# A causal mask added by VectorE in PSUM, in place of two masking products on TensorE

## What is computed

```python
s = jnp.einsum('bnqkgd,bnpkd->bnkgqp', qb, kw, preferred_element_type=F32) * SCALE
...
mask = (diff >= 0) & (diff < WINDOW) & (tk[:, None, :] >= 0)
s = jnp.where(mask[None, :, None, None], s, NEG)
p = jax.nn.softmax(s, axis=-1)
return jnp.einsum('bnkgqp,bnpkd->bnqkgd', p, vw.astype(F32)).reshape(B, S, H, dh)
```

## Time and profile before

| what | value |
|---|---|
| median of 3 runs | 555.83 us (555.33 to 557.75) |
| the profiled execution | 555.62 us, of which the span from first to last instruction is 553.8 us |
| granted TensorE clock over the span | 0.998 |
| TensorE busy | 539.1 us, 97% of the span |
| VectorE busy | 394.7 us, 71% |
| ScalarE busy | 294.2 us, 53% |
| attention, first layer | from about 134 us to 250 us of the span |
| attention, second layer | from about 398 us to 532 us |

### The profile page before, as it was taken

The page is one execution under the profiler, slowest core; times in us unless marked ns, Lnnn a source line. Parts: engine busy times, 40 slices in busy tenths (PEclk is TensorE's granted clock), DMA queues, the critical chain, the costliest instruction groups (busy, mean ns, idle before and its releaser), DMA issues.

```text
span 553.8 us, 8602 instructions
## 1 busy us (share of the span) xinstructions
PE 539.1 (97%) x3171; PEld 400.8 (72%) x3171; DVE 394.7 (71%) x651; ACT 294.2 (53%) x592; POOL 43.7 (8%) x86
## 2 busy tenths in 40 slices
PE   6999999999999999999999999999999999999995
PEld 5777868778767766668887787777877776776674
DVE  4686996689976778656737499668977687587542
ACT  4847735625755465543634773572475454455532
POOL 3001100130000000000520110013000000000000
PEclk9999999999999999999999999999999999999999
DMA  9858465365111111012333856627422112000013
GB/s 265 222 150 212 97 167 109 79 146 137 51 48 30 38 39 40 5 35 76 79 96 95 212 127 152 125 58 151 98 74 78 39 39 49 28 2 1 1 38 113
DMA packets 92040, 49.91 MB, mean 90 GB/s; under 512 B 40912, under 2 KB 90208, under 8 KB 92000
## 3 DMA queue, kind: packets, MB, share of 16 engines
q1 hardware_dynamic: 89376, 45.17, 32.2%
q0 software_dynamic: 1536, 3.15, 2.3%
q10 hardware_dynamic: 1088, 1.06, 0.6%
HBM read 44.12 MB, written 2.10 MB: 83 GB/s over the span
## 4 chain that ended last, share of the span: by engine, by line
PE 77%; DVE 13%; issue 4%; ACT 3%; DMA 1%; POOL 1%; POOLq 0%; DVEq 0%; ACTq 0%
PE z_ps L1491 12%; PE z_ps L1493 11%; PE z_ps L1492 11%; PE t_ps L1591 7%; PE s_ps L1567 6%; PE o_ps L1627 5%; PE a_ps L1627 4%; PE o_ps L1491 3%; PE o_ps L1493 3%; PE o_ps L1492 3%; DVE w_lo L1119 2%; DVE probs L1273 2%; PE t_ps L1601 1%; PE t_ps L1596 1%; DMA swp<-E 1%
## 5 line engine op out<-in xcount | busy, mean ns | idle before, releaser
L1055 ACT ACTIVATE probs<-s_ps,mn 128x128 f32<-128x128 f32 (+3 forms) x128 | 66.6, 526 | 72.1 <-DVE mn L1389 70.7
L1491 PE MATMUL z_ps<-h_hi,w_hi 128*128 128x512 f32 x248 | 101.5, 409 | 1.3 <-issue 0.9
L1493 PE MATMUL z_ps<-h_hi,w_lo 128*128 128x512 f32 x248 | 97.0, 391 | 0.0
L1492 PE MATMUL z_ps<-h_lo,w_hi 128*128 128x512 f32 x248 | 96.8, 390 | 0.0
L900 ACT ACTIVATE w_hi<-stage 128x1024 fp32r<-128x1024 f32 x56 | 59.2, 1058 | 58.7 <-PE z_ps L1493 36.2
L1119 DVE TENSOR_TENSOR w_lo<-stage,w_hi 128x1024 fp32r<-128x1024 f32 x56 | 68.3, 1220 | 7.8 <-ACT w_hi L900 7.0
L1389 DVE TENSOR_REDUCE mn<-s_ps 128x1 f32<-128x384 f32 (+3 forms) x88 | 52.3, 635 | 28.1 <-PE s_ps L1575 27.9
L1491 PEld LDWEIGHTS z_ps<-h_hi,w_hi 128*128 128x128 f32 x248 | 46.6, 188 | 15.5 <-issue 5.5
L1493 PEld LDWEIGHTS z_ps<-h_hi,w_lo 128*128 128x128 f32 x248 | 46.6, 188 | 10.2
L1492 PEld LDWEIGHTS z_ps<-h_lo,w_hi 128*128 128x128 f32 x248 | 46.7, 188 | 8.5 <-issue 0.2
L1398 DVE COPY probsT<-t_ps 128x512 f32<-128x512 f32 (+1 forms) x48 | 32.8, 684 | 22.1 <-PE t_ps L1591 21.8
(11 more groups left out here) (235 smaller groups left out, 915.2 us busy)
## 6 DMA issues: line engine op xcount, KB each, us to landing
stage<-in_w_in SPq DMA_DIRECT2D x28, 512.0 KB, 4.5
stage<-in_w_in SPq DMA_DIRECT2D x32, 256.0 KB, 3.8
stage<-in_cmp_k_w SPq DMA_DIRECT2D x8, 512.0 KB, 3.8
stage<-in_cmp_v_w SPq DMA_DIRECT2D x8, 512.0 KB, 4.2
stage<-in_w_out SPq DMA_DIRECT2D x8, 512.0 KB, 3.5
stage<-in_w_out SPq DMA_DIRECT2D x16, 256.0 KB, 3.8
swp<-E POOLq DMA_DIRECT2D x48, 64.0 KB, 2.3
out<-xT SPq DMA_DIRECT2D x8, 256.0 KB, 2.4
```

Source lines behind the costliest of these rows:

```text
L1055: act.activation(probs[:, 4 * pair + 2 * g + r, c0:c0 + W], s_ps[g][:, at * W:(at + 1) * W], ACT.Exp, scale=-1.0, bias=mn[:, m % 2, g, at: ...
L1491: pe.matmul(bank, w_hi[:, slot, at:at + P], x_hi, start=first, stop=False)
L1492: pe.matmul(bank, w_hi[:, slot, at:at + P], x_lo, start=False, stop=False)
L1493: ins = pe.matmul(bank, w_lo[:, slot, at:at + P], x_hi, start=False, stop=last)
```

## The change

The masking products leave the score step. The last of the three score products now closes the bank and signals VectorE. VectorE adds a table `causal` (128 by 128 float32, zero up to the diagonal and 1e30 beyond) to the last 128 columns of every head in the bank, in place in PSUM, waits for this by a `link`, and then takes the minimum as before. GpSimd builds one table in place of four half tables.

```diff
-        ident_b, causal_b = sb("ident_b", [P, 2, P], BF16), sb("causal_b", [P, 2, P], BF16)
+        causal = sb("causal", [P, P])
...
-        N_CONST = 7
+        N_CONST = 8
...
-            link(pool.memset(ident_b[:, :, :], 0.0))
-            for h in range(2):
-                rows = slice(h * HD, (h + 1) * HD)
-                link(pool.affine_select(out=ident_b[rows, :, :], in_=ident_b[rows, :, :], compare_op=ALU.not_equal, fill=1.0, base=0,
-                                        pattern=[[HD, 2], [-1, P]], channel_multiplier=1))
...
-            link(pool.memset(causal_b[:, :, :], 0.0))
-
-            for h in range(2):
-                rows = slice(h * HD, (h + 1) * HD)
-                link(pool.affine_select(out=causal_b[rows, :, :], in_=causal_b[rows, :, :], compare_op=ALU.is_ge, fill=BIG, base=0,
-                                        pattern=[[HD, 2], [-1, P]], channel_multiplier=1))
+            link(pool.memset(causal[:, :], 0.0))
+
+            pool.affine_select(out=causal[:, :], in_=causal[:, :], compare_op=ALU.is_ge, fill=BIG, base=0,
+                               pattern=[[-1, P]], channel_multiplier=1).then_inc(consts, 1)
...
                 elif kind == "MX":
                     _, l, step, g = st
                     m, many, W = step_no[(l, *step)], len(parts(step)), P * (step[0] + 1)
+                    if g == 0 and m == 0:
+                        dve.wait_ge(consts, N_CONST)
                     if g == 0 and m >= 2:
                         dve.wait_ge(exp_ok, plan.exps[m - 1])
                     dve.wait_ge(s_full, N_KV * m + g + 1)
+                    on_diag = s_ps[g][:, 0:many * W].rearrange("p (h w) -> p h w", h=many)[:, :, W - P:W]
+                    later = causal[:, :].rearrange("p (h c) -> p h c", h=1).to_broadcast([P, many, P])
+                    link(dve.tensor_tensor(on_diag, on_diag, later, ALU.add))
...
-                            pe.matmul(s_ps[g][:, at * wide:(at + 1) * wide], q_st[rows, GROUP * of_q + q, i * P:(i + 1) * P],
-                                      keys, start=(at == 0 and part == 0), stop=False, skip_group_check=True)
-
-                for a in range(2):
-                    for g in range(N_KV):
-                        rows = slice(g * HD, (g + 1) * HD)
-                        diagonal = s_ps[g][:, 0:many * W].rearrange("p (h w) -> p h w", h=many)[:, :, W - P + a * HD:W]
-                        later = causal_b[rows, a, a * HD:P].rearrange("p (h c) -> p h c", h=1).to_broadcast([HD, many, P - a * HD])
-                        ins = pe.matmul(diagonal, ident_b[rows, a, :], later, start=False, stop=(a == 1),
-                                  skip_group_check=True)
-                        if a == 1:
-                            ins.then_inc(s_full, 1)
+                            ins = pe.matmul(s_ps[g][:, at * wide:(at + 1) * wide], q_st[rows, GROUP * of_q + q, i * P:(i + 1) * P],
+                                            keys, start=(at == 0 and part == 0), stop=(part == 2), skip_group_check=True)
+                            if part == 2 and at == len(heads) - 1:
+                                ins.then_inc(s_full, 1)
```

More of the change, by code:

```diff
@@ L1559, in scores @@
                     pe.wait_ge(rope_lo, last + 1)
-                many, wide = len(parts(step)), len(branches) * W
+                wide = len(branches) * W
                 for at, (pair, r) in enumerate(heads):
```

## The result

The changed kernel takes 564.99 us (median of 4 runs, 563.07 to 566.62) against 556.39 us for the kernel before in the same session (4 runs, 555.33 to 557.75). The ratio is 1.015 with an interval of 1.013 to 1.017: slower by 8.6 us, where 5.5 us were forecast. The one run of the changed kernel at a granted clock of 0.999 took 563.07 us; the three other runs, at 0.992 to 0.995, took 564.43 to 566.62.

The account below looks back on a forecast made before the run. TensorE, 97% busy, was taken to bound the kernel, with VectorE nearly full in attention. Stalls of 11.1 us less 5.6 us saved make 5.5 us slower: 555.6 + 5.5 = 561.1 us, range 555 to 567 us.

Parts of the forecast that it names:

- TensorE's saving: Masking products gone from 44 score steps: 0.09, 0.17 or 0.33 us a step by block, 5.6 us in all.
- rival A: The addition is hidden and TensorE keeps its saving, 7.8 us saved against 3 us of stalls: 551 us, chance 0.10.
- The price of an addition: 88 VectorE additions before the minima: 0.32, 0.46 or 0.72 us each with the link, 34 us of new work.
- Rival D: Addition in place in one PSUM bank is slow, some 17 us more VectorE work: 566 to 570 us, chance 0.17.
- rival B: A draw: lateness absorbed, stalls 5 to 8 us, or a free semaphore shortens additions: 557 us, chance 0.20 (0.05 semaphore).
- Where the addition is hidden: Third and fourth block: in some 20 of 32 steps the addition costs nothing and the step gains 0.09 us.
- Where it is not: Score steps without slack and stretches where VectorE is full: four kinds of stalls, 11.1 us in all.
- (4): From the minima at 458.47, the group output delays the second exponential by two additions: 0.6 us.
- (3): Three stretches in blocks 2 and 3 where group outputs fill VectorE: stalls of 1.0, 0.9 and 0.9 us.
- (1): Four score steps of one block whose successors have little or no slack behind the exponentials: some 1.2 us.
- (2): VectorE runs without gap from a minimum to an awaited copy or minimum: 4.4 us first layer, 2.1 us second.
- its own band: The forecast's own case: stalls of 8.5 to 14 us, giving 558.6 to 564 us, chance 0.53.

Follow-up runs that it names:

- seventh experiment: Kernel before, with VectorE additions replacing masking products in only 20 of the 32 score steps of blocks 2 and 3: 554.48 us against 556.45, ratio 0.9955.
- eighth experiment: Kernel before, with the addition on VectorE in one step alone, the last of block 1 in the second layer: 557.31 us beside 558.16, one run.
- sixth experiment: Kernel before, masking products kept, plus two linked VectorE reductions with unread results behind each step's second minimum: 566.61 us, ratio 1.016.
- fifth: Changed kernel with both additions first, then both minima, one link in place of two per step: 564.57 us, ratio 1.013 to the kernel before.

## Why the prediction was nearly right, and where it was not

- **TensorE's saving** was right: 0.10, 0.19 and about 0.31 us a step against 0.09, 0.17 and 0.33, in all 5.9 against 5.6 us, and 5.6 us with no mask at all. The passage between half and full rows stays, as the Trainium skill's "TensorEngine Tiling (Array Packing)", section Key Properties, has it; rival A's extra saving isn't there.
- **The price of an addition** was right: 292, 425 and 694 ns. Rival D (a slow addition in place) fell with that. The part of rival B that rested on a free semaphore fell too: a linked addition is followed by its minimum 0.33 us after it started, its whole length and 0.03 us more, and VectorE's busy time rose by 30 us, as forecast (424.6 us, 75%). By the Trainium skill's "VectorE: DVE Perf Modes", section The DRAIN you can't avoid, the link would cost nothing extra; the rows differ. The unlinked addition at 168.22 takes 0.68 us and its successor starts 0.60 us later, 0.08 before its end; behind a linked one of 0.30 us it starts 0.33 us later, 0.03 after its end.
- **Where the addition is hidden** was right: 20 steps of blocks 2 and 3 can have it for nothing, as the seventh experiment shows by its time.
- **Where it is not**: the group output (4) came within 0.1 us of its size and the stretches (3) within 0.2 in sum (each is about 0.2 off, one of them the other way), and (1) was 0.5 us too high. The first layer's stretch (2) came out at 4.4 us, in part by luck. The prediction has the copy at its end 3.7 us late and TensorE 3.1, which don't fit together, since the second half of the value products starts as soon as that copy is done. Measured, with the 0.9 us of the start taken off, the copy (165.11 before, 168.82 now) is 2.8 us late, and TensorE 3.0 behind one further wait of 0.2 us. The step that was mis-sized is the second layer's stretch of (2), 3.15 us in place of 2.1. Of that, 0.83 us is the last step of block 1, which, by the record of the eighth experiment, was judged by the slack of the next score step and not by that of the tile copy and the value products before it; the eighth experiment shows this by itself. The sixth experiment shows that much of the price, 45% to two thirds, is VectorE's fullness and not the addition's place.
- **What the sum left out**: 2.5 us that stand in no addition's wait. The prediction was summed against one profiled execution in which TensorE's clock rose early: its first products of 128 columns start 0.21 us apart until 5.08 us, and 0.11 from there. In that of the changed kernel the change comes at 7.5. Of the nine other profiled executions the two without this delay are no mask at all and the additions in blocks 2 and 3; the rest reach attention 0.8 to 1.5 us later than the one before, whatever their masks (in the fifth and sixth experiments with a stretch at half the clock from about 13 to 16 us as well). The kernel before, too, ran up to 3.2 us over the profiled one (555.48 to 558.82 us in the two sessions). And a stretch of 3.41 us at half the clock cost 1.6 us, some 1.0 net.

That brings 5.5 us to 8.8: 1.0 more in waits, 0.3 less for the saving, 0.9 at the start, 1.6 for the clock, 0.1 not assigned. The absolute forecast, 561 us with its own band of 558.6 to 564, was missed by the median of 564.99 by a little; the stalls, 12.1 us, lie inside the 8.5 to 14 that went with that band. Where the clock did not fall, the run at 563.07 us lies inside it too, 6.4 to 7.1 us over the runs of before at the same granted clock (556.02 to 556.68, in the other sessions), and the 12.7 us of waits less 5.9 saved make 6.8.

## What to carry to other kernels

Before work is moved to an engine that is busy for 70 to 80% of the span, follow its queue from the place of the new work to the first instruction that anyone waits for, whatever it is: a copy three operations later is a deadline as much as the result itself. Judge a repeated edit step by step: the same kind of edit costs 0.70 us in one step and gains 0.10 us in another, and made in the steps with room alone it turned 8.6 us lost into 2.0 us gained. And a saving on the engine that waits is not simply added to the cost on the one that it waits for; where the second sets the pace, the first is lost (1.6 of 5.9 us here).

## What the runs showed of the hardware

VectorE adds to a PSUM bank in place at the price of an ordinary addition: 292 ns for 128 columns, 425 for 256, 694 for 512, or 1.05 ns a column and some 157 ns. The Trainium skill, "VectorE: DVE Perf Modes", section The TRN2 errata, gives a float32 addition of N elements as (N + 151) / 0.96 ns, which is 291, 424 and 691 ns; the rows, in place in PSUM, agree within 1%.

TensorE can fall to half its clock (1.2 GHz) in the middle of attention. In the changed kernel its products then start 0.43 us apart in place of 0.23:

```profile
207.16 0.63 PE L1490 MATMUL z_ps<-y_lo,w_hi 128*128 128x512 f32 x1
207.58 0.63 PE L1491 MATMUL z_ps<-y_hi,w_lo 128*128 128x512 f32 x1
208.01 0.63 PE L1489 MATMUL z_ps<-y_hi,w_hi 128*128 128x512 f32 x1
```

Of the ten kernels profiled here, five show such stretches within attention, six stretches in all, each beginning 0.4 to 2 us after the end of a wait of TensorE of 0.56 to 1.6 us. All five are kernels in which VectorE's new work makes TensorE wait in blocks 0 and 1; the kernel before, the one without masks, and those with additions in blocks 2 and 3, in the chosen steps and in the single step show none. But most waits of that length were followed by none (in the kernel with additions in blocks 2 and 3, waits of 0.71, 1.61 and 1.22 us), and the kernel before, too, has runs with a lower mean clock (0.991 and 0.992, 558.2 to 558.8 us). That the waits bring the stretches on is possible and not shown, so it is open whether 1.6 us of the 8.8 belong to the change, and the 0.9 us at the start are not put down to it at all.
